# A two-layer decoder step: the low halves of the first layer's weights move from VectorE to GpSimd, the sums of a head move behind all its projections, and GpSimd's order in the attention layer changes

## What is computed

```python
def run_trunk(x, S0s, past_k, past_v, ...):
    h = x
    for l in range(2):
        if l == 0:                                   # HGRN2 layer, 8 heads of 128
            y, S = hgrn2_mixer(rmsnorm(h, g_mix[l]), w_in_a[l], lb_all[l], g_onorm_a[l], w_out_a[l], S0s[l])
            h = h + y
        else:                                        # stick-breaking attention, 16 heads of 64
            k_new, v_new = split(rmsnorm(h, g_kv) @ w_kv, 2)
            q = rmsnorm(h, g_mix[l]) @ w_q_b[0]
            o = stick_breaking_blocked(q, k_all, v_all, sb_bias[0], past_len)
            h = h + o @ w_out_b[0]
        h = h + sq_relu_mlp(rmsnorm(h, g_mlp[l]), w_up[l], w_down[l])
    return rmsnorm(h, g_final), S, k_new, v_new

def hgrn2_mixer(xn, w_in, lb, g_onorm, w_out, S0):
    q, fz, iv, og = jnp.split(xn @ w_in, 4, axis=-1)  # the four projections of a head
    # per head: k, v, log_f from fz and iv; decayed products over chunks, the state S, the output o
    o = o * lax.rsqrt(jnp.mean(o * o, axis=-1, keepdims=True) + EPS)
    o = o.reshape(B, L, D_MODEL) * g_onorm * jax.nn.silu(og)
    return o @ w_out, S_fin
```

## Time and profile before

| | |
|---|---|
| median of 3 runs | 1636.04 us (1634.13 to 1637.82) |
| the profiled execution | 1634.13 us, span 1632.3 us |
| mean granted TensorE clock | 0.991 |
| PE / PEld busy | 1589.9 us (97%) / 1513.7 us (93%) |
| DVE / ACT / POOL busy | 692.2 / 647.2 / 439.6 us (42% / 40% / 27%) |
| the eight heads of the first layer | about 44.7 to 351.5 us; one head takes 38.6 us |
| the attention pairs | about 882 to 1150 us; one pair takes 33.95 us |

### The profile page before, as it was taken

How to read it: one execution, slowest core, us unless ns; L and a number is a source line. 1 busy time by engine, 2 the same in 40 slices (tenths; PEclk the granted TensorE clock), 3 DMA queues, 4 the chain that set the end, 5 groups by cost and what they waited for, 6 DMA issues and landing times.

```text
span 1632.3 us, 35070 instructions
## 1 busy us (share of the span) xinstructions
PE 1589.9 (97%) x13749; PEld 1513.7 (93%) x13749; DVE 692.2 (42%) x1332; ACT 647.2 (40%) x980; POOL 439.6 (27%) x386
## 2 busy tenths in 40 slices
PE   8999999989999999999999999999999999999996
PEld 7899898979999999999998888887999999999995
DVE  7866666653211212112335887888432121121223
ACT  6444444433312313123334776678333131231321
POOL 3000000013333443334341212111434433344330
PEclk9999999999999999999999999999999999999997
DMA  6133232222232222322235654553222223222211
GB/s 176 52 86 98 63 98 81 84 69 78 78 104 77 78 77 77 103 77 77 77 92 188 205 167 144 173 179 104 78 78 78 77 77 103 77 77 77 77 51 58
DMA packets 169516, 158.09 MB, mean 97 GB/s; under 512 B 5389, under 2 KB 160085, under 8 KB 169429
## 3 DMA queue, kind: packets, MB, share of 16 engines
q1 hardware_dynamic: 151490, 147.87, 28.4%
q10 hardware_dynamic: 17938, 8.95, 2.0%
HBM read 145.00 MB, written 11.80 MB: 96 GB/s over the span
## 4 chain that ended last, share of the span: by engine, by line
PE 76%; DVE 1%; ACT 0%; issue 0%; DMA 0%; DVEq 0%; ACTq 0%
PE acc L1788 58%; PE acc L2069 6%; PE pM L2127 3%; PE pL L2110 1%; PE acc L2184 1%; PE pO L2141 1%; PE pO L2173 1%; PE acc L2201 1%; PE acc L2173 1%; PE acc L2263 1%; DVE nrm L1762 0%; PE acc L2273 0%; DMA out_dram<-yrow 0%; PE pL L1853 0%; PE pL L2080 0%
## 5 line engine op out<-in xcount | busy, mean ns | idle before, releaser
L467 POOL TENSOR_TENSOR wlo<-wraw,whi 128x512 fp32r<-128x512 f32 x292 | 371.3, 1304 | 922.5 <-ACT whi L559 922.5
L1788 PE MATMUL acc<-xa_hi,whi 128*128 128x288 f32 x1568 | 344.9, 302 | 0.0
L1788 PE MATMUL acc<-xa_hi,wlo 128*128 128x288 f32 x1568 | 336.2, 296 | 0.0
L1788 PE MATMUL acc<-xa_lo,whi 128*128 128x288 f32 x1568 | 336.0, 296 | 0.0
L559 ACT ACTIVATE whi<-wraw 128x2048 fp32r<-128x2048 f32 x90 | 172.1, 1912 | 327.9 <-PE acc L1788 322.1
L1788 PE MATMUL acc<-xb_hi,whi 128*128 128x288 f32 x1328 | 287.5, 298 | 4.8 <-DVE xb_lo L1034 4.8
L1788 PE MATMUL acc<-xb_lo,whi 128*128 128x288 f32 x1328 | 285.3, 297 | 0.0
L1788 PE MATMUL acc<-xb_hi,wlo 128*128 128x288 f32 x1328 | 285.3, 297 | 0.0
L1788 PEld LDWEIGHTS acc<-xa_hi,whi 128*128 128x128 f32 x1568 | 251.2, 189 | 7.9 <-issue 5.3
L1788 PEld LDWEIGHTS acc<-xa_hi,wlo 128*128 128x128 f32 x1568 | 253.0, 189 | 0.0
L1788 PEld LDWEIGHTS acc<-xa_lo,whi 128*128 128x128 f32 x1568 | 252.5, 189 | 0.0
(11 more groups left out here) (335 smaller groups left out, 1977.3 us busy)
## 6 DMA issues: line engine op xcount, KB each, us to landing
wraw<-in_w_up_dram SPq DMA_DIRECT2D x64, 512.0 KB, 4.4
wraw<-in_w_down_dram SPq DMA_DIRECT2D x64, 512.0 KB, 4.0
Kp<-in_cache_k_dram SPq DMA_DIRECT2D x32, 512.0 KB, 4.3
Vp<-in_cache_v_dram SPq DMA_DIRECT2D x32, 512.0 KB, 5.0
wraw<-in_w_in_a_dram SPq DMA_DIRECT2D x30, 512.0 KB, 5.8
wraw<-in_w_kv_dram SPq DMA_DIRECT2D x16, 512.0 KB, 4.4
St<-in_state_hgrn_dram ACTq DMA_DIRECT2D x8, 512.0 KB, 7.5
out_dram<-Sn ACTq DMA_DIRECT2D x8, 512.0 KB, 4.5
```

Of the source, the lines that this page charges most:

```text
L467: ins = pool.tensor_tensor(wlo[s][:, k:k + 2, :], wraw[s][:, k:k + 2, :], whi[s][:, k:k + 2, :].bitcast(F32), ALU.subtract)
L1788: last = pe.matmul(acc[a][:, hf, 0:HALF], w[s][:, k, a * P:(a + 1) * P], x[:, k, hf * HALF:(hf + 1) * HALF], start=(k == 0 and n == 0), st ...
```

## The change

Three edits, in one change.

1. VectorE's `panel_low` goes from the head loop, in three places (two per head, and one at the end of the last head). GpSimd makes the low halves of panels 3 to 17 instead, with `split_low_panel`; it begins when panels 0 to 2 are done. Panels 1 and 2 stay on VectorE, ahead of the loop.
2. In TensorE's head order the table has other numbers. Level 3 and level 5 stand one k step later, `chunk_states`, `sample_states` and `outputs` too, and the two k steps behind `out_sums` now stand ahead of it, so that `out_sums` is the last step of a head.
3. In the attention loop GpSimd makes `masked_bias(j)` first, and then both units of the low halves; before, the mask stood between the two. Ahead of the loop and behind it the same is done.

```diff
@@ GpSimd
-            pool.wait_ge(lo_done, U_OUT // 2 + 2)
-            split_low(U_OUT // 2 + 2, U_OB // 2)
+            pool.wait_ge(lo_done, 3)
+            split_low_panel(1, 3)
+            split_low(4, U_OB // 2)
...
-            kv_low(0, 0)
-            kv_low(0, 1)
-            kv_low(1, 0)
+            kv_low(0)
             pool.wait_ge(unit_done, U_OB)
             masked_bias(0)
-            kv_low(1, 1)
+            kv_low(1)
             with pool.Fori(1, NPAIR - 1) as j:
-                kv_low(j + 1, 0)
                 masked_bias(j)
-                kv_low(j + 1, 1)
-            kv_low(NPAIR, 0)
+                kv_low(j + 1)
             masked_bias(NPAIR - 1)
+            pool.wait_ge(kv_hi, 2 * NPAIR + 1)
+            split_low_unit(0).then_inc(kv_lo, 1)
@@ VectorE, head()
                 if products:
                     level_into_A(p, 1)
-                if par is not None:
-                    panel_low(1, 2 * h + 1)
-                if products:
                     fold(p, pp, 0)
...
                     sample_states(p)
-                if par is not None:
-                    panel_low(0, 2 * h + 2)
-                else:
-                    panel_low(1, 2 * h + 1)
@@ TensorE
                 fill(at[13], at[14])
                 out_sums(p)
-                fill(at[14], at[15])
...
-            HEAD_AT = [0, 3, 5, 8, 11, 13, 16, 18, 21, 24, 25, 26, 27, 28, 30, 32]
+            HEAD_AT = [0, 3, 5, 8, 11, 14, 16, 19, 21, 24, 26, 27, 28, 30, 32]
```

More of the change, by code:

```diff
@@ L518, in split_low_unit, with kv_low @@
                 return ins
-            def kv_low(j, a):
-                pool.wait_ge(kv_hi, 2 * j + a + 1)
-                split_low_unit(a).then_inc(kv_lo, 1)
+            def kv_low(j):
+                for a in range(2):
+                    pool.wait_ge(kv_hi, 2 * j + a + 1)
+                    split_low_unit(a).then_inc(kv_lo, 1)
             def masked_bias(j):
@@ L2018, in out_fill @@
                     unit_part(0, a, U_OUT // 2, xb_hi, xb_lo, X_HG, k, k + 1)
-            head_products(NB - 1, 1, out_fill, [0, 2, 3, 4, 5, 6, 7, 8, 9, 10, 11, 12, 13, 13, 14, 14])
+            head_products(NB - 1, 1, out_fill, [0, 2, 3, 4, 5, 6, 7, 8, 9, 10, 11, 12, 13, 13, 14])
             for a in range(2):
```

## The result

The changed kernel took 1655.76 us (median of 4 runs, 1654.32 to 1657.12), the kernel before beside it 1636.93 (1634.13 to 1638.3): ratio 1.0117, 95% interval 1.01 to 1.0135. That is 18.8 us slower, where I had forecast 10.5. The profiled execution took 1653.42 us, with a span of 1651.6 us, 19.3 more than before.

What follows compares the result with a forecast made beforehand. TensorE, busy for 97% of the span, was taken as the bound. Terms of 1.6 + 1.8 + 3.6 + 3.5 = 10.5 us on 1634.13 gave 1644.6, stated as 1646.5 for the median; own range 1640 to 1655 us, chance 0.52.

Steps and rivals of the forecast that it cites:

- the fourth rival: Heads: low halves come too late and TensorE waits; needs 7 us delay in one panel; 0.05 left for all others.
- The step that failed: Heads' folds: GpSimd enters only where VectorE waits or reads PSUM, each time holding the next two-input instruction up to 1.27 us.
- second rival: Heads: GpSimd gets between any two VectorE instructions, a fold's three too; 3 us per middle head, 1663 us; chance 0.12.
- one quiet case: Lines 1479 and 1483: VectorE ran 0.60 us apart at usual length while GpSimd's two subtractions took 3.66 us.
- Middle heads, 1.6 us forecast: Six middle heads: fold 5's Q comes late, so level 6 loads 0.27 us later in each; bounds 0 and 3.0 per head.
- The table, 0 us forecast: TensorE's head order: all 32 k steps remain and no middle wait needs filling, so 0 us by itself.
- third rival: Head loop's two turns: different work ahead of the branch changes the 2.8 us stands, up to 5.6 us faster, 1631; chance 0.11.
- The turns, 0 us forecast: Head loop's two turns: no term in the sum; a change of the 2.8 us stands was left to the third rival.
- First head, 1.8 forecast: First head: held folds add about 0.9 us at level 3 and again at level 6; bounds 0 and 2.5.
- Pairs, 3.5 forecast: Attention, 7 pairs: `u_low` waits for GpSimd's low half behind the mask, sums 0.5 us later each; bounds 0 and 0.9.
- Last head, 3.6 forecast: Last head: four meetings of GpSimd and VectorE, 1.15, 1.0 and twice about 0.75 us; bounds 0.5 and 5.1.
- The forecast's upper end of 1655: Whole kernel: top of the forecast's own range, all terms near their upper bounds except the middle heads'.

Runs made afterwards that it cites:

- the runs with reads and with writes: Kernel before plus four unneeded GpSimd instructions at each of 15 high halves: 128x512 subtractions took 1646.84 us, memsets 1635.08 us.
- the run with twelve subtractions: Kernel before plus twelve unneeded GpSimd subtractions of 128x512 at each of 15 high halves: 1731.64 us, one run.
- edit 2 alone: Kernel before with only the new table of k steps, sums last in a head: 1640.35 us, ratio 1.0027.
- edit 1 alone: Kernel before with only the low halves of panels 3 to 17 moved to GpSimd, old table and attention order: 1645.99 us, ratio 1.0064.
- the fine pieces: Changed kernel with each low half of panels 3 to 17 in eight pieces of 128x256, not four of 128x512: 1645.32 us, ratio 1.0057.
- the levels put back: Changed kernel with the k steps between the levels as before, three ahead of level 6, sums still last: 1647.69 us, ratio 1.0076.

## Why the prediction was wrong, step by step

**Right: the direction, and that GpSimd's reads hold VectorE.** The changed kernel is slower, and the runs with reads and with writes show what the meetings cost. In the middle heads TensorE had waited for nothing of VectorE's before, so taking VectorE's 34.3 us away could buy nothing there directly; what it bought by way of a load stands under the turns. The low halves were in time (TensorE waited for none), so the fourth rival fell.

**The step that failed: "GpSimd gets in between only where VectorE waits or reads PSUM", read from the earlier trace rows.** In the changed kernel, and in the run with twelve subtractions, it got in between the three instructions of a fold: beside a panel's subtractions K was held for 0.7 to 1.0 us, Q and the totals for 1.1 each. That was my second rival's mechanism, with a chance of 0.12; its price of 3 us a head was too high, it is 1.8 (10.8 over six). I had laid one quiet case over the one place where three such instructions follow each other. The case itself is still there in the changed kernel (GpSimd's subtraction takes 2.42 us and two of VectorE's pass at usual length), `Sn<-St,tot` in the run with twelve is a second one, and I have no run that explains either.

**Middle heads, 1.6 us forecast.** The folds cost TensorE 10.8 us: 3.6 at level 1, which I had left out, and 7.2 at level 6.

**The table, 0 us forecast.** Wrong twice. It has only two k steps between level 5 and level 6, where there were three. Nobody waited there before, so I priced the cover it takes away at my own small delay of Q (0.27 us a head). With the true delay it was 1.2 a head; putting the steps back saved 6.7 us. And at the turns, with the sums last, 14 matmuls of 2.31 us stood behind the branch's start and not 19 of 2.98: edit 2 alone made the stands 3.8 and 3.7 us. This is the sign opposite to my third rival's. A part of the last head's loss is the table's too, 1.8 us in the run with edit 2 alone.

**The turns, 0 us forecast.** I knew of the 2.8 us stands and looked for their cause in what TensorE does. The shorter stands of the changed kernel (1.3 and 1.5 us, -2.7 us, and no lower clock behind them, about -1.4) came from edit 1, by way of the load of slot 0. I had even written that this slot comes free 10 us earlier, and that the DMAs are no issue.

**First head, 1.8 forecast,** 2.9 measured, by the same failed step: Qs of 1.5 us there too. **Pairs, 3.5 forecast,** 3.9 measured, by the path I gave.

**Last head, 3.6 forecast,** 6.2 measured. TensorE's waits at the first levels grew from 1.2 to 4.5 us, by 3.3, close to the term. The rest is the clock. The last head before and after:

```profile
325.30:351.70 26.40, 24.97 (x392) 21.39 (x391) 18.34 (x48) 9.52 (x21) 0.00 (x0) 1.00 0.18 51
```

```profile
336.20:368.80 32.60, 27.96 (x393) 24.09 (x391) 19.36 (x47) 10.82 (x23) 5.63 (x4) 0.84 0.23 68
```

The same matmuls took 3.0 us more at a mean granted clock of 0.84. Every kernel that waited longer in this stretch showed it (0.94 with edit 1 alone and with edit 2 alone, 0.89 with the fine pieces), and those that waited as before had 1.00. How low it falls does not go by the wait alone: with the levels put back TensorE waited 5.2 us there, longer than in the changed kernel, at 0.89. I had no term for it.

**The sum.** 10.5 became +2.9, +7.6 (10.8 of held folds, less 2.7 and 1.4 at the turns, and 0.9 that I did not trace), +6.2 and +3.9: 20.6, less 1.3 in the untouched stretches, is the 19.3 of the two spans. Against the forecast the failed step, the cover and the clock are the largest parts. (The forecast's upper end of 1655 also lay above its own terms: 1.6 + 2.5 + 5.1 + 6.3 is 15.5 us, which gives 1651.5.)

## What to carry to other kernels

In these runs work that moved to GpSimd was paid for by nearly each VectorE instruction with two SBUF inputs beside it, up to one GpSimd instruction each. So cut it small or let it only write, and count the held instructions in a chain, not the first alone. A wait that a table of order covers does not show in the profile; before a step loses cover, ask what delay the same change puts on what it waits for. Where an engine stands at a loop's branch for no reason that the profile names, look at what the DMAs do at that moment, and at the instruction queue among them: here one wait that moved a load by 8 us gave the best kernel of all.

## What the runs showed that I had not expected

- A branch back over a loop body of two heads took 3.3 to 3.9 us with the DMA idle (share 0.03), 5.4 to 5.9 with a 1 MB load under way, and 6.4 to 6.6 with the load begun just ahead of it. The packet of code started 0.9 to 1.1, 2.8 to 3.4 and 3.8 to 4.0 us behind the branch's start.
- With GpSimd reading all the time, a product of 8 columns took 1.00 us on VectorE: what is paid is GpSimd's instruction, not one's own.
- In pieces of 128x256 the panels cost 10 us less in the whole kernel than in pieces of 128x512, and in one piece some 17 more.
- TensorE waited 3.3 us more at the levels of the last head, and lost another 3.0 there by the clock.
